# Forgetting attention in a hybrid encoder trunk: in odd steps TensorE issues the output products ahead of the transposes

## The chip, the cores and the metric

The program runs on one core of one Trainium2 chip. The time is the device time of one launch in microseconds (us), lower is better. The kernel before was timed in three runs.

## The reference, cut to what matters

Two layers over 1024 prompt tokens and 32 new tokens, width 1024. In each layer one input projection feeds sliding-window attention and forgetting attention ("FoX") with 8 heads of width 64; then come an output projection and an MLP. All of it is float32. The part that the change touches is the FoX attention of the prompt:

```python
def fox_prompt(q, k, v, logf):
    F = jnp.cumsum(logf, axis=1)
    def block(args):                      # one block of 128 queries
        qi, Fi, i = args
        s = jnp.einsum('bqhd,bkhd->bhqk', qi, k) * SCALE
        s = s + Fi[..., None] - Fk[:, :, None, :]
        s = jnp.where(kpos[None, :] <= qpos[:, None], s, -jnp.inf)
        p = jax.nn.softmax(s, axis=-1)
        return jnp.einsum('bhqk,bkhd->bqhd', p, v)
```

## The kernel before

The program is written out by hand: each engine has its own instruction stream, executed in the order written, and the streams meet only in semaphores. Float32 matrices are split into a rounded high part and a remainder, so one product is three matmuls (high x high, high x low, low x high). The names end in h and l (`pth`, `ptl`, `fvh`, `fvl`).

The FoX stage of a layer handles its 8 heads in 4 pairs (`fox_pair(t, first, last)`, t = 0 to 3; t = 1 and 2 are one hardware loop). A pair has 16 steps e: steps 0 to 7 for the first head, 8 to 15 for the second. The query block of a step is `FOX_ORDER[e % 8]` with `FOX_ORDER = [6, 7, 4, 5, 2, 3, 0, 1]`; a block i sees i + 1 key blocks of 128. For one step the work is:

- TensorE, `fox_scores` (L1764 to L1766): the scores, into one or two PSUM banks of banks 0 to 3. At step e the scores of step e + 2 are issued. They wait until the exponential of step e has read the banks.
- VectorE, `fox_max` (L1307): the row maximum. ScalarE, `fox_expo` (L807): the exponential into `pbuf`, and a read of the accumulated sum.
- TensorE, `p_transposes` (L1793): the i + 1 tiles of `pbuf` are transposed, up to four tiles to a group, and each group fills PSUM bank 4 or 5 in turn. Steps with i of 4 and more have two groups, the others one. Group g waits until VectorE has finished group g - 2 (`ft_lo`), which used the same bank.
- ScalarE, `pt_hi` (L585, `pth`): the high part of each group, copied out of PSUM. VectorE, `pt_lo` (L1370, `ptl`): the remainder.
- TensorE, `products` (L1829): out = v times p for two query blocks at once (256 columns). A product set jj belongs to the steps 2jj and 2jj + 1 of the pair and comes in two halves: half 0 is issued at step 2jj + 2, half 1 at step 2jj + 3. Only half 0 waits, for `ptl` of step 2jj + 1:

```python
if part == 0:
    pe.wait_ge(sm("ft_lo"), pr * NFT + BT[2 * jj + 1] + NBT[2 * jj + 1])
```

A half has J + 1 key blocks of three matmuls, J = 3, 2, 1, 0 for jj = 0 to 3 and again for jj = 4 to 7: 12, 9, 6 or 3 matmuls. At steps 0 and 1 the last set of the pair before is issued. So at step 3 TensorE issues half 1 of set 0 (12 matmuls), at step 4 half 0 of set 1 (9 matmuls), which needs the `ptl` of step 3.

VectorE runs `pt_lo(e - 1)`, then `fox_max(e + 2)`, at each step e, and at some steps a remainder for operands of the scores behind them (`stack_lo`, L1295 and L1298) or for v (L1400, `fvl`, at step 1). ScalarE runs `fox_expo(e + 1)`, then `pt_hi(e)`, and at some steps a copy for the same operands. At step 14 and at the next pair's step 0, `spreads` (L1805) broadcasts the inverse sums through a bank of the same two, and VectorE copies it out (L1350) and normalises (L1360). After the last pair POOL makes the last remainder `hl` (L543), for which the output projection waits.

Of the kernel before, what the change touches and what calls it, by code (L numbers as in the profile page):

```python
# [72 lines left out]
def build(nc, a):  # L73
    ctx = ExitStack()
    with ctx:
# [145 lines left out]
        def sm(name):  # L221
            if name not in S:
                S[name] = sem(name)
            return S[name]

        def wait_apart(e, held, *waits):

            for name, v in (held, *waits):  # L230
                if isinstance(v, int):
                    if v > 0:
                        e.wait_ge(sm(name), v)
                else:
                    e.wait_ge(sm(name), v)
# [347 lines left out]
        def _(act):  # L583
# [66 lines left out]
            for l in range(DEPTH):  # L650
# [23 lines left out]
                for q, it in enumerate(PJ):  # L674
                    b = q % 4
                    if by_act(it):
                        act.wait_ge(sm("pj_mm"), l * NPJ + q + 1)
                    if it[0] == "f":
                        _, blk, j, c = it
                        dst = (kf, qf)[blk // 2]  # L680
                        copy(dst[:, 2 * (blk % 2) + j, c * CH:(c + 1) * CH], ps[:, b, 0:CH], scale=SCALE if blk >= 2 else 1.0).then_inc(sm("ev_act"), 1)
# [4 lines left out]
                        if l and q == 4:  # L686
                            pre_hi(l, NPRE1, 2)
                    else:
                        _, u, i = it

                        if u == U_GATE:
# [856 lines left out]
        def _(pe):  # L1548
            def three(out, w_hi, w_lo, m_hi, m_lo, k, nk, start=True, stop=True):

                pe.matmul(out, w_hi, m_hi, start=start and k == 0, stop=False)  # L1551
                pe.matmul(out, w_hi, m_lo, start=False, stop=False)  # L1552
                return pe.matmul(out, w_lo, m_hi, start=False, stop=stop and k == nk - 1)  # L1553
# [30 lines left out]
            def modulate(out, halves):  # L1584

                for k in range(KT):
                    w = halves[k // 4][:, (k % 4) * 512:(k % 4 + 1) * 512]
                    for g in range(4):
                        ins = pe.matmul(out[32 * g:32 * g + 32, :], scp[:, k, :], w[:, g * P:(g + 1) * P], start=(k == 0), stop=(k == KT - 1),  # L1589
                                        skip_group_check=True)  # L1590
                ins.then_inc(sm("ada_mm"), 1)

            def mod_columns(out, rows):

                pick = ident[:, :].rearrange("p (g n) -> p g n", g=4)[:, :, 0:2]
                return pe.matmul(out, rows, pick, start=True, stop=True, skip_group_check=True)

            for l in range(DEPTH):
# [123 lines left out]
                def p_transposes(w):  # L1722
                    W = P if w % 8 == 0 else 256
                    pe.wait_ge(sm("s_norm"), l * 16 + w + 1)
                    pe.wait_ge(sm("st_lo"), l * 16 + w)
                    for kb in range(W // P):
                        for hd in range(4):
                            ins = pe.transpose(ps[:, 4 + kb, hd * P:(hd + 1) * P], pbuf[w % 2][:, hd * W + kb * P:hd * W + (kb + 1) * P], ident[:, :])  # L1728
                    ins.then_inc(sm("st_mm"), 1)

                def products(w):
                    g, i = w // 8, w % 8
                    if w >= 2:
                        pe.wait_ge(sm("so_lo"), l * 16 + w - 1)

                    if w % 2:
                        for i_ in range(2):
                            pe.wait_ge(sm(f"ada_v_in{i_}"), (l * NB2 + w // 2 + 1) * 16)
                        modulate(ps[:, 7, 256:256 + P], ada_v)
                    pe.wait_ge(sm("st_lo"), l * 16 + w + 1)  # L1740
                    pe.wait_ge(sm("sv_lo"), l * 2 + g + 1)
                    kbs = [0] if i == 0 else [i - 1, i]
                    todo = [(kb, d) for kb in range(len(kbs)) for d in range(2)]
                    for x, (kb, d) in enumerate(todo):
                        vsl = slice(64 * d, 64 * d + P)
                        out = ps[:, 6 + w % 2, 0:256]
                        ins = three(out, svh[:, kbs[kb], vsl], svl[:, kbs[kb], vsl],
                                    spth[w % 2][:, kb, 2 * d:2 * d + 2, :], sptl[w % 2][:, kb, 2 * d:2 * d + 2, :], x, len(todo))
                    ins.then_inc(sm("so_mm"), 1)

                def fox_scores(t, e, first=False):
                    pr = l * 4 + t
                    h, i = e // 8, FOX_ORDER[e % 8]
                    n, nb = (i + 1) * P, (1 if i < 4 else 2)
                    w = n // nb
                    if e % 8 == 0:
                        pe.wait_ge(sm("fq_lo"), pr * 4 + 2 * h + 2)
                        pe.wait_ge(sm("fq_hi"), pr * 3 + 2 * h + 1)
                        pe.wait_ge(sm(f"frow_in{h}"), (pr + 1) * 32)
                    pe.wait_ge(sm("fs_exp"), pr * 16 + (max(0, e - 1) if first else e - 1))  # L1760
                    qb = slice(i * P, (i + 1) * P)
                    for c in range(nb):
                        out = ps[:, 2 * (e % 2) + c, 0:w]
                        pe.matmul(out, q1[h][:, qb], k1[h][:, c * w:(c + 1) * w], start=True, stop=False)  # L1764
                        pe.matmul(out, q2[h][0:68, qb], k2[h][0:68, c * w:(c + 1) * w], start=False, stop=(c < nb - 1))  # L1765
                    pe.matmul(ps[:, 2 * (e % 2) + nb - 1, w - P:w], identb, causb, start=False, stop=True).then_inc(sm("fs_mm"), 1)  # L1766
# [29 lines left out]
                def spreads(t, b):  # L1796

                    pr = l * 4 + t
                    g = (BT[R0_AT] - 1, BT[16])[b]
                    pe.wait_ge(sm("fs_rd"), pr * 2 + b + 1)  # L1800
                    pe.wait_ge(sm("ft_lo"), pr * NFT + g - 1)
                    for x in range(4):
                        i = 4 - 4 * b + x
                        for h in range(2):
                            ins = pe.matmul(ps[64 * h:64 * h + 64, 4 + g % 2, x * P:(x + 1) * P], rinv[:, h, i:i + 1].broadcast_to([P, 64]), ident[:, :],  # L1805
                                            start=True, stop=True, skip_group_check=True)
                    ins.then_inc(sm("ft_mm"), 1)
# [25 lines left out]
                def fox_pair(t, first, last):  # L1833
                    for e in range(16):
                        if e < 14:
                            fox_scores(t, e + 2, first and e == 0)
                        elif not last:
                            fox_scores(t + 1, e - 14)
                        if e == 0 and not first:
                            spreads(t - 1, 1)  # L1840
                        if e == R0_AT:
                            spreads(t, 0)
                        if e == 0 and first:
                            wait_apart(pe, ("zero_ok", 1), ("so_lo", (l + 1) * 16), ("fz_ok", 5 * (l + 1)))
                            for b in range(NB2):
                                ins = mod_columns(ps[:, 7, 8 * b:8 * b + 8], mrow[:, b * P:(b + 1) * P])
                            ins.then_inc(sm("mod_mm"), 1)
                        p_transposes(t, e, first)
                        if e >= 2:
                            products(t, e // 2 - 1, e % 2, first)  # L1850
                        elif not first:
                            products(t - 1, 7, e)

                fox_pair(0, True, False)
                with pe.Fori(1, 3) as t:
                    fox_pair(t, False, False)
                fox_pair(3, False, True)
                products(3, 7, 0)
                spreads(3, 1)
# [257 lines left out]
```

## Time and profile before

| | us |
|---|---|
| median of three runs | 3067.51 (3062.65 to 3069.81) |
| the profiled execution | 3068.11 |
| its span, first to last instruction | 3066.0 |
| TensorE (PE) busy | 2903.3 |
| VectorE (DVE) busy | 1317.5 |
| ScalarE (ACT) busy | 965.5 |
| mean granted TensorE clock | 0.96 of full speed |

The FoX stages lie at about 458 to 637 us (layer 0) and 1960 to 2142 us (layer 1). A matmul's duration in the rows includes its way through the array, so consecutive matmuls overlap; the difference of two starts tells what one really takes of TensorE. "PEld" rows are weight loads.

### The profile page before, as it was taken

To read this page: it belongs to the slowest core of one execution; us is meant where nothing else is said; L and a number is where in the kernel's file an instruction comes from. 1 tells how busy PE (TensorE), PEld (TensorE's weight loads), DVE (VectorE), ACT (ScalarE), POOL (GpSimd) and SP (SyncE) were. 2 spreads that over 40 slices of the span, in tenths; PEclk is the share of its full clock that TensorE was granted. 3 is DMA by queue.
4 is the path that set the end of the run, shared out by engine and by line. 5 is a ranking of instruction groups with operands and counts; after the bars stand their busy time and mean duration, and the time that the engine had idled before them with its cause. 6 is when DMAs were issued, how large, how long until landed. Compare 5 with 4: busy or idle time off the path is not lost.

```text
span 3066.0 us, 48014 instructions
## 1 busy us (share of the span) xinstructions
PE 2903.3 (95%) x19587; PEld 2729.6 (89%) x19587; DVE 1317.5 (43%) x2393; ACT 965.5 (31%) x1948; POOL 85.2 (3%) x87
## 2 busy tenths in 40 slices
PE   6999888899999999999999988888999999999997
PEld 5998667789999999999989976777989999999997
DVE  3113667733633333333361347677164333333334
ACT  4222446633411122211242235566152221111222
POOL 0000001100000000000000000111000000000000
PEclk8999689999999999999999988899999999999999
DMA  8111230031211111111211113201221111111121
GB/s 289 42 57 37 80 137 2 18 112 65 102 42 55 63 60 55 41 57 66 110 66 56 45 57 111 84 2 60 97 84 42 42 55 41 42 54 41 41 85 57
DMA packets 135344, 203.31 MB, mean 66 GB/s; under 512 B 8352, under 2 KB 90320, under 8 KB 134672
## 3 DMA queue, kind: packets, MB, share of 16 engines
q1 hardware_dynamic: 135200, 201.27, 19.0%
q8 instruction: 105, 1.72, 0.2%
q14 instruction: 39, 0.32, 0.0%
HBM read 170.45 MB, written 31.00 MB: 66 GB/s over the span
## 4 chain that ended last, share of the span: by engine, by line
PE 87%; DVE 4%; ACT 3%; issue 2%; DMA 1%; DVEq 0%; POOL 0%; POOLq 0%; ACTq 0%; SPq 0%
PE ps L1551 23%; PE ps L1553 23%; PE ps L1552 23%; PE ps L1581 3%; PE ps L1829 3%; PE ps L1793 2%; PE ps L1589 2%; PE ps L1719 1%; PE ps L1728 1%; PE ps L1718 1%; PE ps L1764 1%; DMA ada_v<-w_ada 1%; PE ps L1765 1%; PE ps L1713 1%; DVE st L1307 1%
## 5 line engine op out<-in xcount | busy, mean ns | idle before, releaser
L1551 PE MATMUL ps<-hh,wh 128*128 128x352 f32 x2304 | 758.0, 329 | 15.4 <-DVE wl L1069 11.0
L1553 PE MATMUL ps<-hh,wl 128*128 128x352 f32 x2304 | 745.9, 324 | 0.0
L1552 PE MATMUL ps<-hl,wh 128*128 128x352 f32 x2304 | 744.6, 323 | 0.0
L1551 PE MATMUL ps<-uh,wh 128*128 128x352 f32 x1536 | 500.2, 326 | 4.1 <-DVE modn L1501 2.6
L1552 PE MATMUL ps<-ul,wh 128*128 128x352 f32 x1536 | 493.0, 321 | 0.0
L1553 PE MATMUL ps<-uh,wl 128*128 128x352 f32 x1536 | 493.0, 321 | 0.0
L1551 PEld LDWEIGHTS ps<-hh,wh 128*128 128x128 f32 x2304 | 437.1, 190 | 21.6 <-DVE wl L1069 11.0
L1552 PEld LDWEIGHTS ps<-hl,wh 128*128 128x128 f32 x2304 | 438.2, 190 | 1.3
L1553 PEld LDWEIGHTS ps<-hh,wl 128*128 128x128 f32 x2304 | 437.2, 190 | 0.0
L585 ACT ACTIVATE wh<-raw 128x2048 fp32r<-128x2048 f32 (+1 forms) x90 | 172.0, 1911 | 582.6 <-PE ps L1930 581.0
L1069 DVE TENSOR_TENSOR wl<-raw,wh 128x2048 fp32r<-128x2048 f32 (+1 forms) x90 | 207.5, 2306 | 324.2 <-ACT wh L585 324.2
L1514 DVE TENSOR_TENSOR y<-ps,y 128x352 f32<-128x352 f32 x336 | 173.4, 523 | 363.6 <-PE ps L1553 363.3
L1551 PEld LDWEIGHTS ps<-uh,wh 128*128 128x128 f32 x1536 | 288.7, 188 | 6.6 <-DVE ul L1480 4.0
L1552 PEld LDWEIGHTS ps<-ul,wh 128*128 128x128 f32 x1536 | 288.9, 188 | 0.5
L1475 DVE TENSOR_TENSOR u_t<-r_t 128x352 f32<-128x352 f32 x192 | 100.8, 525 | 436.6 <-ACT r_t L997 434.6
L1553 PEld LDWEIGHTS ps<-uh,wl 128*128 128x128 f32 x1536 | 288.1, 188 | 0.0
L997 ACT ACTIVATE r_t<-ps 128x352 f32<-128x352 f32 x192 | 89.2, 465 | 515.5 <-PE ps L1553 515.5
L1551 PE MATMUL ps<-wh,hh 128*128 128x256 f32 (+1 forms) x720 | 209.1, 290 | 0.0
L1552 PE MATMUL ps<-wl,hh 128*128 128x256 f32 (+1 forms) x720 | 204.7, 284 | 0.0
L1553 PE MATMUL ps<-wh,hl 128*128 128x256 f32 (+1 forms) x720 | 203.9, 283 | 0.0
L1551 PEld LDWEIGHTS ps<-wh,hh 128*128 128x128 f32 x720 | 137.2, 190 | 0.4 <-issue 0.4
L1553 PEld LDWEIGHTS ps<-wh,hl 128*128 128x128 f32 x720 | 137.4, 191 | 0.0
(254 smaller groups left out, 3852.6 us busy)
## 6 DMA issues: line engine op xcount, KB each, us to landing
ada_v<-w_ada SPq DMA_DIRECT2D x32, 1024.0 KB, 7.3
raw<-w_up SPq DMA_DIRECT2D x32, 1024.0 KB, 5.1
raw<-w_down SPq DMA_DIRECT2D x32, 1024.0 KB, 5.0
raw<-w_in SPq DMA_DIRECT2D x16, 1024.0 KB, 5.4
x_kept<-xr SPq DMA_DIRECT2D x6, 1408.0 KB, 9.4
xf<-x_kept SPq DMA_DIRECT2D x2, 4224.0 KB, 13.5
x_kept<-xf SPq DMA_DIRECT2D x6, 1408.0 KB, 5.5
xr<-x_kept SPq DMA_DIRECT2D x2, 4224.0 KB, 14.0
```

Of the source, the lines that this page charges most:

```text
L585: return act.activation(out, in_, ACT.Copy, **kw)
L997: act.activation(r_t[q % 2][:, :], ps[:, q % 4, 0:CH], ACT.Relu).then_inc(sm("u_relu"), 1)
L1069: dve.tensor_tensor(wl[slot(l, n)][:, 0:w], raw[slot(l, n)][:, 0:w], wh[slot(l, n)][:, 0:w].bitcast(F32), ALU.subtract).then_inc(sm("w_lo" ...
L1475: dve.tensor_tensor(u_t[q % 2][:, :], r_t[q % 2][:, :], r_t[q % 2][:, :], ALU.mult).then_inc(sm("u_sq"), 1)
L1514: dve.tensor_tensor(y[:, kt, cs], ps[:, DB[last][q], 0:CH], y[:, kt, cs], ALU.add).then_inc(sm("d_add"), 1)
L1551: pe.matmul(out, w_hi, m_hi, start=start and k == 0, stop=False)
L1552: pe.matmul(out, w_hi, m_lo, start=False, stop=False)
L1553: return pe.matmul(out, w_lo, m_hi, start=False, stop=stop and k == nk - 1)
L1581: ins = pe.matmul(ps[:, 4 + s, 0:CH], onesd[:, :], sq[:, k, c * CH:(c + 1) * CH], start=(k == 0), stop=(k == KT - 1))
L1589: ins = pe.matmul(out[32 * g:32 * g + 32, :], scp[:, k, :], w[:, g * P:(g + 1) * P], start=(k == 0), stop=(k == KT - 1), skip_group_check= ...
L1793: ins = pe.transpose(ps[:, 4 + g % 2, (kb - k0) * P:(kb - k0 + 1) * P], pbuf[e % 2][:, kb * P:(kb + 1) * P], ident[:, :])
L1829: ins = pe.matmul(out, wv[:, kb, vsl], mv, start=False, stop=(kb == 2 * J + 1 and wv is fvl), skip_group_check=True)
```

## The change

In a step with odd e, `products` is issued ahead of `p_transposes`; in even steps the order stays. Nothing else changes: no instruction, buffer or wait is added or removed, and the other engines' streams are the same.

```diff
-                        p_transposes(t, e, first)
+                        if e % 2 == 0:
+                            p_transposes(t, e, first)
                         if e >= 2:
                             products(t, e // 2 - 1, e % 2, first)
                         elif not first:
                             products(t - 1, 7, e)
+                        if e % 2:
+                            p_transposes(t, e, first)
```

## Rows read from the trace of the kernel before

**Rows 1.** The page: engines' busy time, and the granted clock in 40 slices.

```profile
PE 2903.3 (95%) x19587; PEld 2729.6 (89%) x19587; DVE 1317.5 (43%) x2393; ACT 965.5 (31%) x1948; POOL 85.2 (3%) x87
...
PEclk8999689999999999999999988899999999999999
```

**Rows 2.** Windows, the stretch of layer 0's FoX stage: length, busy of each engine, clock.

```profile
457.70:637.00 179.30, 153.08 (x1172) 134.15 (x1172) 127.00 (x205) 111.08 (x245) 28.45 (x26) 0.95 0.06 20
```

**Rows 3.** Waits within one pair (545.2 to 590.1): total, times, longest.

```profile
PE ps L1793 <- DVE ptl L1370: 4.8, 3, 3.2
```

**Rows 4.** Timeline of PE, steps 3 and 4: start, duration, instruction.

```profile
562.77 0.83 PE L1793 MATMUL ps<-ident,pbuf 128*128 128x128 f32 x6
...
563.36 0.37 PE L1829 MATMUL ps<-pth,fvh 128*128 128x256 f32 x1
...
564.79 0.28 PE L1764 MATMUL ps<-k1a,q1a 128*128 128x128 f32 x1
...
565.34 0.36 PE L1829 MATMUL ps<-pth,fvh 128*128 128x256 f32 x1
```

**Rows 5.** Timeline of ScalarE and VectorE in the same two steps.

```profile
563.42 0.87 ACT L585 ACTIVATE pth<-ps 128x512 fp32r<-128x512 f32 x2 [1.67 <-PE ps L1793]
...
564.05 1.02 DVE L1370 TENSOR_TENSOR ptl<-ps,pth 128x512 fp32r<-128x512 f32 x2 [0.38 <-ACT pth L585]
```

**Rows 6.** Timeline, steps 11 and 12 of the same pair.

```profile
582.49 0.83 PE L1793 MATMUL ps<-ident,pbuf 128*128 128x128 f32 x6
...
583.77 1.02 DVE L1370 TENSOR_TENSOR ptl<-ps,pth 128x512 fp32r<-128x512 f32 x2 [0.38 <-ACT pth L585]
...
585.06 0.36 PE L1829 MATMUL ps<-pth,fvh 128*128 128x256 f32 x1
```

**Rows 7.** Timeline, steps 1 and 2 of the same pair.

```profile
552.89 1.05 PE L1793 MATMUL ps<-ident,pbuf 128*128 128x128 f32 x8
...
554.34 1.08 ACT L585 ACTIVATE pth<-ps 128x512 fp32r<-128x512 f32 x2
...
555.29 1.06 ACT L585 ACTIVATE fvh<-vf 128x1024 fp32r x1
...
556.51 1.23 DVE L1400 TENSOR_TENSOR fvl<-vf,fvh 128x1024 fp32r<-128x1024 f32 x1 [2.46 <-ACT fvh L585]
...
558.39 1.07 PE L1793 MATMUL ps<-ident,pbuf 128*128 128x128 f32 x5 [3.20 <-DVE ptl L1370]
```

**Rows 8.** Timeline, steps 5 and 6 of the same pair.

```profile
567.00 0.42 DVE L1307 TENSOR_REDUCE st<-ps 128x1 f32<-128x256 f32 x1 [0.29 <-PE ps L1766]
...
567.45 1.69 DVE L1298 TENSOR_TENSOR k2b<-kf,k1b 64x1024 fp32r<-64x1024 f32 x1
...
569.47 0.47 PE L1764 MATMUL ps<-k1b,q1b 128*128 128x448 f32 x1 [1.07 <-DVE k2b L1298]
```

**Rows 9.** Timeline, ScalarE at steps 7 and 8 of the same pair.

```profile
572.96 0.39 ACT L585 ACTIVATE pth<-ps 128x256 fp32r<-128x256 f32 x1
...
573.99 1.12 ACT L807 ACTIVATE pbuf<-ps,st 128x1024 f32<-128x1024 f32 x1 [0.65 <-DVE st L1307]
```

**Rows 10.** Timeline, the end of layer 1's last pair, steps 13 to 15 and after.

```profile
2132.29 0.69 DVE L1370 TENSOR_TENSOR ptl<-ps,pth 128x512 fp32r<-128x512 f32 x1 [0.71 <-ACT pth L585]
...
2133.50 0.33 PE L1793 MATMUL ps<-ident,pbuf 128*128 128x128 f32 x1
...
2135.38 0.42 DVE L1370 TENSOR_TENSOR ptl<-ps,pth 128x256 fp32r<-128x256 f32 x1
...
2135.86 0.39 PE L1829 MATMUL ps<-pth,fvh 128*128 128x256 f32 x1 [0.35 <-DVE ptl L1370]
```

**Rows 11.** Windows: twice after the 3.20 us wait, and after that of 1.07.

```profile
559.60:561.00 1.40, 1.40 (x8) 1.32 (x7) 1.37 (x2) 1.38 (x3) 0.00 (x0) 0.50 0.00 0
562.20:564.00 1.80, 1.80 (x16) 1.53 (x15) 0.69 (x1) 0.58 (x2) 0.00 (x0) 1.00 0.00 0
569.50:571.00 1.50, 1.50 (x9) 1.21 (x10) 0.70 (x2) 0.22 (x1) 1.50 (x2) 1.00 0.00 0
```

## The prediction

> **What bounds the kernel now.** I read the page first: TensorE is busy 2903.3 of 3066.0 us, at a clock near full speed [rows 1]. So the kernel is bound by TensorE's order of work, and a change that adds or removes no instruction can act only through TensorE's idle time. Then I read the FoX stage by windows: TensorE is busy 153.08 of 179.3 us there, with VectorE at 127.00 and ScalarE at 111.08 [rows 2]; no engine is full, so the stage is bound by hand-overs between the three. The waits of one pair say which: 4.8 us in three waits of transposes for `ptl`, one of them 3.2 us [rows 3]. Last I read the timeline of that pair step by step, since a reorder is decided by which hand-over has slack. The reader is to see in it where the three stand: 3.2 us and 1.4 us at steps 2 and 10, where the order does not change, and the rest of the 4.8, 0.2 us, at step 9; the other odd steps run from scores through transposes to products without a gap.
>
> **What the order does now.** At step 3 the six transposes start at 562.77 and the 12 product matmuls at 563.36; the next scores start at 564.79, three transposes of step 4 follow, and the products of step 4 start at 565.34 [rows 4]. Those need `ptl` of step 3. ScalarE starts its copies at 563.42 and VectorE's subtractions run from 564.05 to 564.05 + 1.02 = 565.07 [rows 5]. So the way from the first transpose to the last `ptl` is 565.07 - 562.77 = 2.30 us, and TensorE fills it with the 12 matmuls, which take 564.79 - 563.36 = 1.43 us.
>
> **The change, term by term.** After the change the 12 matmuls come ahead, so the transposes start 1.43 us later and nothing long stands between them and the products that need their result.
>
> *Steps 3 to 4.* The hand-over from `ptl` to the matmul that waits for it takes 0.06 us where TensorE was waiting (products at 2135.86 after a wait of 0.35, `ptl` done at 2135.38 + 0.42 = 2135.80 [rows 10]). So half 0 of set 1 may start 2.30 + 0.06 = 2.36 us after the first transpose of step 3. TensorE has for that time the transposes (563.36 - 562.77 = 0.59), and the scores with the transposes of step 4 (565.34 - 564.79 = 0.55), 1.14 us in all. It idles 2.36 - 1.14 = 1.22 us, where now it idles none. Put the other way: 1.43 us of delay less the present slack of 565.34 - 565.13 = 0.21 us. Most of the idle time will stand ahead of the transposes of step 4, since these wait for the first of step 3's two groups.
>
> *Steps 11 to 12* are the same with the other head: transposes at 582.49, `ptl` done at 583.77 + 1.02 = 584.79, products at 585.06 [rows 6]. The way is again 2.30 us and the slack 0.21, so again 1.22 us. Each pair of each layer has both places: 2 x 4 x 2 = 16 places, 16 x 1.22 = 19.5 us.
>
> *Steps 5 to 6.* The transposes of step 5 come later by the nine matmuls ahead of them (three quarters of 1.43, 1.07 us). VectorE is meanwhile at `k2b`, which follows the row maximum of step 7's scores, from 567.45 to 569.14 [rows 8]; `ptl` of step 5 waits behind it in VectorE's order and is not late. Cost nothing. If that cover were gone, it would be about 1 us in 8 places. But `k2b` does not absorb the delay of step 4 either: it begins where the row maximum ends, and that waits for scores which stand behind the delayed products. The 1.07 us wait [rows 8] is pushed back whole, as are the POOL casts and the two small transfers that wait for the same scores.
>
> *Steps 1 to 2.* Three matmuls go ahead of the eight transposes (0.35 us). ScalarE copies the step's groups from 554.34, then `fvh`; VectorE does `fvl`, then `ptl`, and the transposes at 558.39 wait for that [rows 7]. ScalarE is without idle before 554.34, and the transposes, now over at 552.89 + 1.05 = 553.94, would be over at about 554.30. So the 3.20 us wait stays as it is: no gain, no loss.
>
> *Steps 7 to 8.* Six matmuls go ahead (0.7 us). The copy at 572.96 moves to about 573.67, ends at 574.06, and pushes the exponential from 573.99 [rows 9] by 0.07 us, which the next scores wait for. 8 x 0.07 = 0.6 us.
>
> *Steps 9, 13, 15.* At step 9 the wait of 0.2 us is covered by three matmuls, but the next transposes wait for VectorE, whose chain is not moved: they wait that much more. Gain nothing. At 13 and 15 the next pair's scores and the spread stand between, and hide the delay.
>
> *The end of a layer.* In the last pair no scores of a next pair follow. `ptl` of step 13 (now 2132.29 to 2132.98) moves by 1.07 to 2134.05, and the transpose of step 14, now at 2133.50 [rows 10], can start at 2134.11: 0.61 us. Then six matmuls (0.7 us) stand ahead of step 15's two transposes, whose `ptl` the products at 2135.86 already wait for [rows 10]. Together 1.3 us per layer, on the way to the output projection: 2.6 us.
>
> The sum is 19.5 + 0.6 + 2.6 = 22.7 us. The profiled execution took 3068.11 us (span 3066.0), 0.6 us over the median of 3067.51; 3067.5 + 22.7 = 3090.2 us, slower by 0.74%.
>
> **The unknown costs.** How long TensorE takes to resume behind a new wait is bounded from below by nothing, which makes each place 1.16, and from above by 0.33 us, the gap between `k2b`'s end at 569.14 and the scores at 569.47 [rows 8], which makes it 1.49. The first gives 21.7 us, the second 27 us. I take 0.06, since that row is a product matmul that waits for `ptl` alone, while the scores wait for several semaphores. With the small terms uncertain by 2 us, the likeliest case's own range is 3086 to 3096.
>
> **The clock.** After the wait of 3.20 us the granted clock is 0.50, the 1.2 GHz level, and back at 1.00 (2.4 GHz) from 562.20; after the wait of 1.07 us it stays at 1.00 [rows 11]. The new gaps are of the smaller size, so the sum has no term for the clock. The Trainium skill ("TensorE: Matmul & The Clock Gate", section "A second HAM failure mode: psum-queue depth-cycling") speaks against relying on that: in a kernel that cycles through PSUM banks, short idle gaps between groups of matmuls were enough to make the clock go down and up again. By the rows the sum stays at 22.7 us; by that rule the new gaps would bring low stretches of their own, which is the second rival. The row behind the shorter wait does not agree with the rule.
>
> **The rivals.**
>
> *The reorder helps: faster.* The idea is that odd-step transposes are what waits, and that products without a wait should fill it. It would also release `fvh`, which waits until the last set's half 1 is done, earlier by the eight transposes (about 0.9 us), and so shorten the 3.20 us wait in 6 pairs that have a pair before them. That gives at most 6 x 0.9 = 5.4 us, and 1.6 us for the small waits at step 9: 3060.5 us, if at the same time the places at steps 4 and 12 cost nothing. It decides if ScalarE reaches `fvh` before those matmuls end. Against it: `fvh` starts right behind the copies at 555.29, with no idle time [rows 7]. Chance 0.05.
>
> *The clock falls behind the new gaps.* A low stretch lasts from about 558.9 to 562.2, 3.3 us at half speed, which loses 1.65 us [rows 11]. At the 8 places behind step 3, which follow the 3.20 us wait closely: 22.7 + 8 x 1.65 = 35.9, 3103 us; at all 16 places 49.1, 3117 us. For it speaks that the gap comes within 3 us of the clock's return, when only a burst of work lies between; against it the wait of 1.07 us. Chance 0.14.
>
> *The delay is absorbed by the waits that follow.* If `k2b` and the operand remainders did not follow the scores, the 1.07 us wait at step 6 would swallow most of steps 3 to 4, leaving about 0.15 us there, and the gap of some 0.3 us at the pair's start a part of steps 11 to 12, leaving 0.9: 8 x 1.05 + 3.2 = 11.6, 3079 us. Against it: the row maximum at 567.00 waits for TensorE by its own row [rows 8]. Chance 0.07.
>
> *It does nothing.* If the products of even steps were not held by `ptl` as read, or if ScalarE and VectorE took a late group as fast as it came, all would lie within a few us: 3067.5 us. For this the way of 2.30 us would have to shrink to 1.14, below the two engines' own durations of 0.87 and 1.02 us in a row less their overlap [rows 5]. Chance 0.04.
>
> **How the numbers follow.** The likeliest case has 0.70, the clock 0.14, absorbed 0.07, faster 0.05, nothing 0.04. A change of 0.2% is about what a measurement of this kernel can tell from none: 6 us. Slower by more holds 0.70 + 0.14 + 0.07 = 0.91, within it 0.05 (nothing, and half of the faster case, whose size is about the bound), faster 0.04. The range leaves out the faster and nothing cases and the worst clock case: from the absorbed case, 3078, to the clock at 8 places, 3104.
>
> **What the profile after would show.** Right: in each pair, ahead of the transposes of steps 4 and 12, idle time of about 1 us released by `ptl` of L1370, and 0.1 us more ahead of the products; the 3.20 us wait and the 1.07 us wait as before; a pair of 44.8 us grows to about 47.3; the busy time of each engine unchanged; everything outside the FoX stages unchanged. Wrong if the gaps at steps 4 and 12 are much under 1 us, if the wait of 3.20 us shrinks, or if the clock's low stretches grow in number or length.

## The result, and the profile after

Four runs of the changed kernel took 3089.55 to 3098.07 us, median 3096.4; four of the kernel before, beside them, 3062.65 to 3069.81, median 3065.44. The ratio is 1.0098 (95% interval 1.0084 to 1.0111): the change makes the kernel slower by 1.0%, 30 us. The profiled execution has a span of 3094.8 us against 3066.0, 28.8 us more.

The page of the changed kernel, engines' busy time and the granted clock in 40 slices, answers to [rows 1]:

```profile
PE 2913.5 (94%) x19571; PEld 2732.2 (88%) x19587; DVE 1316.4 (43%) x2393; ACT 964.0 (31%) x1948; POOL 85.2 (3%) x87
...
PEclk8999689999999999999999977899999999999999
```

The other engines' busy time is within 1.5 us of before; TensorE's is 10 us higher, and the clock digits are lower where layer 0 turns into layer 1. The windows of layer 0's whole FoX stage, with the stretch up to the output projection's first matmul, answer to [rows 2]:

```profile
457.65:652.15 194.50, 157.99 (x1174) 136.35 (x1182) 128.90 (x206) 113.25 (x248) 31.02 (x27) 0.94 0.06 19
```

Between the same two instructions the stage took 181.49 us before (459.06 to 640.55) and takes 194.50 now; in layer 1 it took 182.30 and takes 194.51. Together that is 25.2 of the 28.8 us. The waits within one pair (501.4 to 548.7), against [rows 3]:

```profile
PE ps L1793 <- DVE ptl L1370: 6.9, 4, 3.2
...
PE ps L1764 <- DVE k2b L1298: 1.0, 1, 1.0
```

The transposes wait for `ptl` 6.9 us in four waits instead of 4.8 in three; the longest is the same. Which wait is new, the timeline of that pair shows, at steps 3 and 4 against [rows 4, 5]:

```profile
520.56 0.84 PE L1793 MATMUL ps<-ident,pbuf 128*128 128x128 f32 x6
521.16 0.31 PE L1764 MATMUL ps<-k1a,q1a 128*128 128x128 f32 x1
...
521.85 1.02 DVE L1370 TENSOR_TENSOR ptl<-ps,pth 128x512 fp32r<-128x512 f32 x2 [2.08 <-ACT pth L585]
...
522.60 0.55 PE L1793 MATMUL ps<-ident,pbuf 128*128 128x128 f32 x3 [0.95 <-DVE ptl L1370]
...
522.93 0.39 PE L1829 MATMUL ps<-pth,fvh 128*128 128x256 f32 x1
```

From step 3's first transpose at 520.56 to the last `ptl` at 521.85 + 1.02 = 522.87 are 2.31 us (2.30 before), and the products start 0.06 us later. Between them TensorE now has only the transposes, the scores and a wait of 0.95 us. Below are the unchanged wait at step 2 and the new one at step 12 ([rows 7, 6]), and from the end of layer 1's last pair ([rows 10]) a new wait of 0.54 us at step 14 and one that has grown from 0.35 to 0.99 us behind step 15:

```profile
514.65 0.93 PE L1793 MATMUL ps<-ident,pbuf 128*128 128x128 f32 x5 [3.21 <-DVE ptl L1370]
...
543.53 0.55 PE L1793 MATMUL ps<-ident,pbuf 128*128 128x128 f32 x3 [0.95 <-DVE ptl L1370]
...
2161.70 0.30 PE L1793 MATMUL ps<-ident,pbuf 128*128 128x128 f32 x1 [0.54 <-DVE ptl L1370]
...
2164.59 0.39 PE L1829 MATMUL ps<-pth,fvh 128*128 128x256 f32 x1 [0.99 <-DVE ptl L1370]
```

Last the clock. Behind the 3.20 us wait the low level lasted 3.4 us in each of the pairs t = 1 to 3 before ([rows 11] show one). In the changed kernel it lasted 6.8 us in t = 2 and 3 of both layers. Windows of t = 2, layer 0, where TensorE resumes at 561.97; the eighth number is the granted clock:

```profile
559.00:560.00 1.00, 0.00 (x0) 0.00 (x0) 0.00 (x0) 1.00 (x2) 0.00 (x0) 1.00 0.00 0
560.00:561.00 1.00, 0.00 (x0) 0.00 (x0) 0.91 (x1) 0.83 (x2) 0.00 (x0) 0.74 0.00 0
...
562.00:564.00 2.00, 2.00 (x8) 1.85 (x10) 1.97 (x3) 0.85 (x3) 0.00 (x0) 0.50 0.00 0
...
566.00:567.00 1.00, 1.00 (x5) 0.48 (x4) 0.00 (x0) 0.00 (x0) 0.00 (x0) 0.50 0.00 0
567.00:568.00 1.00, 1.00 (x9) 1.00 (x9) 0.69 (x1) 0.00 (x0) 0.00 (x0) 0.84 0.00 0
```

The clock falls inside the wait, some 1.5 us before work resumes, and stays low to about 567.3, before the next new gap has come (at 569.7). Before the change it fell in all six pairs t = 1 to 3 as the work resumed or up to 1 us after.

A measure that the experiments share: the time from the transposes of step 2 to those of step 10 (first head, holds the place of steps 3 to 4), and from there to step 2 of the next pair (second head, holds steps 11 to 12). It is a difference of two starts in the timeline.

| kernel, pair | steps 2 to 10 | steps 10 to 2 |
|---|---|---|
| before, t = 1 | 21.49 | 23.34 |
| changed, t = 1 | 22.71 (+1.22) | 24.61 (+1.27) |
| before, t = 2 | 21.38 | 23.18 |
| changed, t = 2, low clock 6.8 us | 23.45 (+2.07) | 24.44 (+1.26) |

### The profile page after: what moved, and what is told of

Read it like the earlier page. It is cut to its first block, busy times and chain, and to the rows that moved or that the text cites. A ratio compares the mean times of both kernels' runs of the same rounds, so it can differ in the third digit from the quotient of the medians.

```text
span 3094.8 us, 47998 instructions
## 1 busy us (share of the span) xinstructions
PE 2913.5 (94%) x19571; PEld 2732.2 (88%) x19587; DVE 1316.4 (43%) x2393; ACT 964.0 (31%) x1948; POOL 85.2 (3%) x87
## 4 chain that ended last, share of the span: by engine, by line
PE 86%; DVE 5%; ACT 3%; issue 2%; DMA 0%; DVEq 0%; POOL 0%; POOLq 0%; ACTq 0%; SPq 0%
PE ps L1551 23%; PE ps L1553 22%; PE ps L1552 22%; PE ps L1581 3%; PE ps L1829 3%; PE ps L1793 2%; PE ps L1719 1%; PE ps L1589 1%; PE ps L1728 1%; PE ps L1718 1%; DVE ptl L1370 1%; PE ps L1764 1%; ACT pth L585 1%; PE ps L1713 1%; PE ps L1765 1%
## 5 line engine op out<-in xcount | busy, mean ns | idle before, releaser
L1551 PE MATMUL ps<-hh,wh 128*128 128x352 f32 x2304 | 758.4, 329 | 14.9 <-DVE wl L1069 11.0
L1793 PE MATMUL ps<-ident,pbuf 128*128 128x128 f32 x576 | 94.4, 289 | 57.7 <-DVE ptl L1370 56.0
```

What stands on the lines that cost most here:

```text
L1793: ins = pe.transpose(ps[:, 4 + g % 2, (kb - k0) * P:(kb - k0 + 1) * P], pbuf[e % 2][:, kb * P:(kb + 1) * P], ident[:, :])
```

## The experiments

All were timed beside the kernel before on the same chip, in two groups; a ratio is to the kernel before of its group (3064.9 and 3065.28 us).

**Steps 3 and 11 alone.**

```diff
-                        p_transposes(t, e, first)
+                        late = e in (3, 11)
+                        if not late:
+                            p_transposes(t, e, first)
                         (products as before)
+                        if late:
+                            p_transposes(t, e, first)
```

> Products ahead of the transposes at steps 3 and 11 alone. Hand-over theory: these are the 16 places that cost (12 matmuls, 1.43 us, less 0.21 us of slack), so 16 x 1.22 = 19.5 us over the kernel before, about 3085 us; in the trace, idle time of about 1.0 us ahead of the transposes of steps 4 and 12. Rival, each odd step costs alike because TensorE loses time at every changed hand-over from one kind of matmul to the other: 2 of 8 steps, so a quarter of the 31 us measured, 8 us. Second rival, most of the 31 us is the granted clock: the time would be within 5 us of before, with the idle time there but the low stretches as before.

Measured: 3080.76 us, ratio 1.0062 (1.0048 to 1.0077), 19 us slower. The halves of pair t = 1 are 22.71 and 24.59, those of the full change. The wait at step 12:

```profile
540.16 0.55 PE L1793 MATMUL ps<-ident,pbuf 128*128 128x128 f32 x3 [0.95 <-DVE ptl L1370]
```

The interval is 15 to 24 us; by the medians it is 16. Both rivals fall, the quarter (8 us) and the clock alone (under 5 us): two of the eight odd steps carry nearly the whole hand-over cost. The low clock behind the 3.20 us wait lasted 6.8 us in five of the six later pairs (in t = 2 of layer 0 the first half is 1.98 us longer than before, not 1.22), so a part of the 19 us is the clock's.

**All odd steps but 3 and 11.**

```diff
+                        late = e % 2 and e not in (3, 11)
```

> Products ahead of the transposes at steps 1, 5, 7, 9, 13 and 15, the order of before at 3 and 11. Hand-over theory: these have cover or slack, except the last pair of a layer (1.3 us each) and 0.07 us at step 7: about 3.2 us over before, 3069 us. Rival of a cost at every changed step: three quarters of 31, 23 us. If the low stretches behind the 3.20 us wait are still as short as before, the longer ones of the changed kernel do not come from these steps.

Measured: 3066.43 us, ratio 1.0013 (1.0004 to 1.0023), 4 us slower. Halves 21.41 and 23.38, as before. The waits of pair t = 1 behind step 3:

```profile
524.33 0.47 PE L1764 MATMUL ps<-k1b,q1b 128*128 128x448 f32 x1 [1.00 <-DVE k2b L1298]
...
534.62 0.92 PE L1793 MATMUL ps<-ident,pbuf 128*128 128x128 f32 x5 [1.76 <-DVE ptl L1370]
```

No wait at steps 4 and 12. At step 10 it is 1.76 us, the old one and what the matmuls of step 9 no longer take up: covering the 0.17 us of step 9 gained nothing, since VectorE's chain was not moved. The 0.07 us forecast for step 7 is not seen: the first halves are 0.04 to 0.10 us shorter than before in layer 0's later pairs. The low clock behind the 3.20 us wait lasted 3.4 us in all six later pairs. But in layer 1, t = 0, the clock fell once more, at 1991.6, just behind the wait at step 10, which is 1.82 us there, and stayed low for 3.4 us; that half took 24.65 us against 23.16 before.

**Half of the matmuls ahead.**

```diff
+                        if e in (3, 11):
+                            products(t, e // 2 - 1, 1, first, (0, 2))   # two key blocks
+                            p_transposes(t, e, first)
+                            products(t, e // 2 - 1, 1, first, (2, 4))   # the other two
+                            continue
```

> At steps 3 and 11, six of the twelve product matmuls go ahead of the transposes and six behind them; all other steps as before. Hand-over theory, in which the delay counts only beyond the slack: six matmuls take about 0.75 us, less 0.21 us of slack is 0.54 us, in 16 places 8.6 us, 3074 us. Rival, any delay of the transposes costs the whole way through ScalarE and VectorE: as steps 3 and 11 in full, 19.5 us. Rival, the six matmuls left behind cover it all: no change.

Measured: 3072.53 us, ratio 1.0022 (1.0011 to 1.0033), 6.7 us slower. The wait at step 4 of pair t = 1:

```profile
522.70 0.55 PE L1793 MATMUL ps<-ident,pbuf 128*128 128x128 f32 x3 [0.27 <-DVE ptl L1370]
```

The second half of pair t = 0 takes 23.81 us against 23.15 before and 24.48 in the full change: +0.66 where twelve matmuls give +1.33; in t = 1 it is +0.61 where they give +1.27, and 0.54 was worked out. So the cost follows the delay less the slack, and both rivals fall: six matmuls cost neither as much as twelve nor nothing.

**The order of before, `fvl` later.** On VectorE the block of `fvl` goes from step 1, where it stood ahead of `pt_lo(t, 1)`, to step 2 behind it:

```diff
-                        if e == 1:
+                        if e == 2:        # now behind pt_lo(t, e - 1)
                             dve.wait_ge(sm("fv_hi"), l * 4 + t + 1)
                             ...
```

> The order of before on TensorE; on VectorE the remainder fvl moves from step 1 to step 2, behind ptl of step 1, which it held back. If the 3.20 us wait at step 2 is only VectorE's order: ptl of step 1 runs at about 555.0 instead of 557.65, the transposes of step 2 wait about 0.6 us, and the products of step 2 then wait for fvl until about 557.7 instead of 559.25: at least 1.5 us in each of 8 pairs, 12 us. If the low clock behind that wait comes from the length of the wait, it goes too (up to 1.65 us each, 13 us more): 3042 us. If the low clock comes from the order of the work and not from the wait, it stays: 3055 us.

Measured: 3042.58 us, ratio 0.993 (0.9917 to 0.9943), 21.5 us faster. The 3.20 us wait has split into two, and in t = 2 of both layers, which have no low clock here, a third appears at step 3:

```profile
546.13 0.93 PE L1793 MATMUL ps<-ident,pbuf 128*128 128x128 f32 x5 [0.52 <-DVE ptl L1370]
...
548.21 0.39 PE L1829 MATMUL ps<-pth,fvh 128*128 128x256 f32 x1 [0.91 <-DVE fvl L1383]
...
551.25 0.88 PE L1793 MATMUL ps<-ident,pbuf 128*128 128x128 f32 x6 [0.82 <-DVE ptl L1370]
```

From step 2 to step 2 of the next pair are 43.34 us (t = 1) where there were 44.83: the 1.5 us expected. Low clock remains in the records at three pairs of the profiled execution, 13.7 us a layer against 17.1 and 20.5, so only a part of it went with the wait. This execution is the slowest of the five.

**The change on top of that.** The same edit of `fvl`, and the changed order.

> The changed order together with the later fvl of the run e4_fvl_later, to be compared with that run. There the transposes of step 3 wait 0.82 us for ptl of step 2, which the 12 matmuls ahead would cover. Hand-over theory: step 3's transposes start 1.43 - 0.98 = 0.45 us later instead of 1.43, less 0.21 of slack is 0.24 us at 6 places (in the two first pairs of a layer 1.22), and 1.22 us at steps 11 to 12 as before: 6 x 0.24 + 2 x 1.22 + 8 x 1.22 + 3.2 = 16.8 us over e4_fvl_later, 3059 us. Rival, the change costs what it cost before, whatever the transposes waited for: 30 us, 3072 us.

Measured: 3066.55 us, ratio 1.0002 (0.999 to 1.0013). Against the run with `fvl` alone (0.993) that is 0.7%, 22 us, with some 5 us of uncertainty; 16.8 was expected. The two groups ran on different chips, so the halves of the pairs are the better witness. Without the change, t = 2 takes 22.15 and 20.62 us; with it 22.39 and 21.88: +0.24 and +1.26, where 0.24 and 1.22 were worked out. In both layers t = 2 is the later pair without low clock in either run. In t = 1 and 3 of layer 0 the run without the change has 3.4 us of low clock and no wait at step 3; with the change the low clock is gone, and their first halves are 0.32 and 0.20 us shorter, not 0.24 longer, while t = 1's second half is again 1.25 longer. So the two FoX stages grew by 11.6 us, less than the 16.8. The two profiled executions differ by 22.6 us, and the other 11.0 lie outside the stages, where the code is the same; whether they are scatter or the other chip is not shown. The timeline, t = 2, shows why:

```profile
554.63 0.39 PE L1829 MATMUL ps<-pth,fvh 128*128 128x256 f32 x1 [0.91 <-DVE fvl L1383]
...
560.15 0.55 PE L1793 MATMUL ps<-ident,pbuf 128*128 128x128 f32 x3 [0.95 <-DVE ptl L1370]
```

The wait of 0.82 us at step 3 is gone, covered by the matmuls, and the one of 0.95 us at step 4 has come for it. The records of its FoX stages show no low clock at all, and the second halves of t = 0 to 2 still take 1.25 to 1.35 us more. So the reorder costs without the clock's help, and even where it covers a real wait.

**Three moves on VectorE.** `fvl` as above, and

```diff
-                        if e in (2, 5):
-                            stack_lo(t, 1, e // 5)
+                        if e in (2, 4):
+                            stack_lo(t, 1, e // 4)
...
-                        if e in (9, 12) and not last:
+                        if e in (10, 12) and not last:
```

> TensorE in the order of before; on VectorE fvl from step 1 to step 2, k2b from step 5 to step 4, and the next pair's q1a from step 9 to step 10. If the waits of 1.07 us at step 6 and of 1.42 us at step 10 are VectorE's order alone, they go: 6 x 1.07 + 2 x 0.33 = 7 us and up to 6 x 0.9 = 5 us under e4_fvl_later, 3031 us. Rival, the remainder moved in holds up the ptl behind it, and the wait only changes its place: 3042 us as in e4_fvl_later.

Measured: 3037.33 us, ratio 0.9904 (0.9892 to 0.9917), 28 us faster than the kernel before, and the fastest here. Pair t = 2, steps 10 and 11:

```profile
566.87 0.93 PE L1793 MATMUL ps<-ident,pbuf 128*128 128x128 f32 x5 [0.19 <-DVE ptl L1370]
...
569.95 0.87 PE L1793 MATMUL ps<-ident,pbuf 128*128 128x128 f32 x6 [0.19 <-DVE ptl L1370]
```

The wait of 1.42 us is 0.19, with 0.19 us new behind it, and the wait for `k2b` is gone. 3031 was expected: some of it is taken by `ptl` of step 10 behind `q1a`, as the rival said.

**The change on the three moves.**

> The changed order on TensorE together with the three moves of e6_three_moves. Hand-over theory: at steps 3 to 4 as in e5_change_on_e4, and at steps 11 to 12 the transposes wait a little for ptl of step 10, behind q1a, which the matmuls ahead cover: between 10 and 17 us over e6_three_moves. Rival, once VectorE's waits are gone the covering order is the better one: under e6_three_moves.

Measured: 3054.82 us, ratio 0.9973 (0.9959 to 0.9987), against 0.9904: 0.7%, 21 us slower than without the change, by the medians 17.5, where 10 to 17 was expected; the FoX stages grew by 14.9 us. The waits of 0.95 us are there at steps 4 and 12:

```profile
552.23 0.55 PE L1793 MATMUL ps<-ident,pbuf 128*128 128x128 f32 x3 [0.95 <-DVE ptl L1370]
...
571.13 0.55 PE L1793 MATMUL ps<-ident,pbuf 128*128 128x128 f32 x3 [0.95 <-DVE ptl L1370]
```

The halves of t = 2 are 20.32 and 21.90 against 19.91 and 21.02. They grew by less than 1.22. Two things in the traces bear on it: without the change the FoX stages have 10.2 and 13.7 us of low clock, 3.4 of them in the first half of this pair, and with it none; and the wait of 0.19 us at step 11 is covered. What each takes was not tried. The rival, that the covering order wins once VectorE's waits are gone, falls.

**A longer pair without a new gap.** This asks where the longer low clock comes from. The order is that of before, and the four transposes of step 13 are issued seven times over.

```diff
-                        for kb in range(k0, k1_):
+                        for kb in list(range(k0, k1_)) * (7 if e == 13 else 1):
```

> The order of before, with the four transposes of step 13 issued seven times over (into the same place), so that each pair is about 2.3 us longer with TensorE busy and without a new gap: 8 x 2.3 = 18.5 us, 3083.5 us, if nothing else changes. It asks for the rest of the 31 us: behind the 3.20 us wait the low clock lasted 3.4 us in all six later pairs of the kernel before, and 6.8 us in four of six in the changed kernel. If that comes from the new gaps at steps 4 and 12, it lasts 3.4 us here in all pairs. If it comes from where in time the wait falls, which any change of a pair's length shifts, it lasts 6.8 us in some pairs here too, and the time is some 3 to 6 us longer, 3087 us.

Measured: 3086.16 us, ratio 1.0069 (1.0052 to 1.0085), 21 us slower; the padding itself measures 2.62 us a pair (25.96 against 23.34), 21 us. Windows of t = 1 in layer 0, where TensorE resumes at 511.53:

```profile
508.50:509.50 1.00, 0.00 (x0) 0.00 (x0) 0.00 (x0) 1.00 (x3) 0.00 (x0) 1.00 0.00 0
509.50:511.50 2.00, 0.00 (x0) 0.00 (x0) 1.86 (x3) 0.88 (x2) 0.00 (x0) 0.53 0.00 0
...
513.00:516.00 3.00, 3.00 (x14) 2.90 (x13) 2.27 (x4) 2.17 (x5) 0.00 (x0) 0.50 0.01 3
516.00:517.00 1.00, 1.00 (x8) 0.53 (x7) 0.25 (x1) 0.00 (x0) 0.00 (x0) 0.78 0.00 0
```

The low level lasts 6.8 us here too, and in five of the six later pairs, with no gap at steps 4 and 12. So the new gaps are not needed for it. Its price shows here too: these five pairs' first halves take 0.5 to 0.8 us more than before, the sixth's 0.1. In the half-ahead run three of six pairs have it, in the same code as the other three. The 3.20 us wait stands in the later pairs of six kernels: before, changed, steps 3 and 11 alone, all but these, half ahead, and this one, 36 pairs in all. In 17 of them the low level lasts 6.8 us, and there the clock fell 0.8 to 2.0 us before TensorE resumed. In 19 it lasts 3.4 us, and there the clock fell between 0.6 us before TensorE resumed and 1.5 us after. What sets the place of the fall was not tried.

## Why the prediction was right

The measured 3096.4 us lies in the range, 6 us over the 3090.2 forecast. Against the kernel before beside it the change costs 30 us (31 by the medians) where 22.7 was forecast, so 7 to 8 us are missing from the sum. One of the prediction's own signs of being wrong came about: the clock's low stretches grew in length. The places and the size of the idle time were right; the clock was not. Step by step:

- *Steps 3 to 4 and 11 to 12*, 1.22 us each. Measured +1.22 and +1.27 in a pair without longer low clock, and the gap ahead of the transposes 0.95 to 1.10. Run alone, these two steps gave 19 us (15 to 24), where 19.5 was the term. The half dose gave 6.7 us where the same working gave 8.6, and the place with 0.82 us to cover gave +0.24 as worked out. The hand-over of 0.06 us held; the bound of 0.33 did not apply.
- *Steps 5, 9, 13* without cost and *steps 1 to 2* without gain: the 3.20 us wait measured 3.17 to 3.21 in every pair, and the 1.07 us wait 1.00. *Step 7* and *the end of a layer*, 3.2 us: the run of the other steps alone gave 4 us (1 to 7), too wide to tell the 0.6 us of step 7, which its halves do not show. From step 10 of the last pair to the output projection the changed kernel takes 20.58 us against 18.02 and 18.05, 2.5 more. The run of steps 3 and 11 alone takes 19.35 there, 1.3 more, and the run of the others 19.28, 1.25 more: that is the end of a layer, for which 1.3 was forecast.
- *The clock*: taken as nothing, this is the term that was mis-sized. The two FoX stages grew by 25.2 us, not 22.7. Low clock in them rose from 17.1 to 23.9 us in layer 0 and from 20.5 to 23.9 in layer 1. In t = 2 the first half grew by 2.07 us where that of t = 1 grew by 1.22, so a longer low stretch cost about 0.85 us, less than the 1.65 of the rival, since a part of it lies inside the wait; in four pairs that makes 3.4 us. The rival had the clock fall anew behind the gaps at steps 4 and 12: it never did. What lengthened was the old low stretch, and the padded run shows that a change of the pair's length is enough.
- *The rest*, 28.8 - 25.2 = 3.6 us, lies outside the FoX stages, where nothing was changed. Span less stages was 2702.2 us before, 2705.8 after, and 2689.4 to 2708.0 in the eight experiments with the same code there, so 3.6 us is within what one execution differs from another. By the same scatter the median of four runs can lie some us off.
- *Faster* and *absorbed* fall with the unchanged 3.20 us wait and with +1.22 and +1.27 in both halves, and *it does nothing* with the 30 us.
- *The chances*: "nothing, and half of the faster case" is 0.04 + 0.025 = 0.065, not 0.05, and the other half 0.025, not 0.04. The sum of the low bound, 16 x 1.16 + 3.2, is 21.8, not 21.7. Neither changes the forecast.

## What to carry to other kernels

Before two blocks of one in-order engine are exchanged, ask of each what waits for its result, and what stands between it and that wait. A block that others need (here transposes, whose result takes 2.3 us through two engines) goes first, and work that nobody waits for is the cover behind it. The cost of the wrong order is the moved work less the slack, per place, and it can be read from one timeline. What the clock adds cannot: here a longer pair alone made some low stretches longer. The waits worth attacking stood on another engine: three remainders moved by a step on VectorE, without touching TensorE, gave 28 us.

## What the runs showed of the hardware that was not expected

- The low clock behind the same wait lasted either 3.4 or 6.8 us, from one pair to the next of one program; in 36 pairs it was 6.8 where it began 0.8 us or more before TensorE resumed, and 3.4 where it began at most 0.6 us before, or later.
- The 16 gaps of 0.95 or 1.10 us ahead of the transposes of steps 4 and 12 brought no low stretch of their own. Of the six waits of 1.8 us at step 10 in t = 0 (two each in the changed kernel, in the changed order with `fvl` later and in the run of all odd steps but 3 and 11) one did.
- Much of the scatter between runs of one program is the clock: of the kernel before, runs with a mean granted clock of 0.963 to 0.964 took 3057.93 to 3063.23 us, those with 0.959 took 3067.33 to 3072.77.
